# A two-block transformer on one core: attention one turn deeper, and the queries' projection ahead of the key compression

## What is computed

```python
def shared_kv(h, positions, kv_norm, kv_w, kc_pe, vc_pe, kc_w1, kc_w2, vc_w1, vc_w2, kc_gain, ks_gain, kw_gain):
    hn = rms_norm_2(h, kv_norm)
    parts = (hn @ kv_w).reshape(B, T, 6, N_KV_GROUPS, HEAD_DIM_2)
    ...
    def compress(raw, pe, w1, w2):
        blk = raw[:, idx] + pe[None, None, :, None, :]
        blk = jnp.moveaxis(blk, 3, 2).reshape(B, n_cmp, N_KV_GROUPS, CMP_LEN * HEAD_DIM_2)
        return jax.nn.gelu(blk @ w1) @ w2
    kc = compress(kc_raw, kc_pe, kc_w1, kc_w2)
    vc = compress(vc_raw, vc_pe, vc_w1, vc_w2)
    kc = partial_rope(rms_norm_2(kc, kc_gain), positions[:, ends])
    ks = partial_rope(rms_norm_2(ks, ks_gain), positions)
    kw = partial_rope(rms_norm_2(kw, kw_gain), positions)
```

## Time and profile before

| | us |
|---|---|
| median of 3 executions | 2927.88 (2927.32 to 2928.37) |
| profiled execution, its own time | 2929.42 |
| its span in the profile | 2927.6 |
| PE busy in the span | 2418.8 (83%) |
| DVE busy | 1984.4 (68%) |
| ACT busy | 1416.6 (48%) |
| PE's share of the chain that ended last | 59% |
| PE's mean granted clock, share of full | 0.879 |

### The profile page before, as it was taken

How to read it: one execution, slowest core, us unless ns; L and a number is a source line. 1 busy time by engine, 2 the same in 40 slices (tenths; PEclk the granted TensorE clock), 3 DMA queues, 4 the chain that set the end, 5 groups by cost and what they waited for, 6 DMA issues and landing times.

```text
span 2927.6 us, 31365 instructions
## 1 busy us (share of the span) xinstructions
PE 2418.8 (83%) x12811; PEld 2054.3 (70%) x12811; DVE 1984.4 (68%) x2430; ACT 1416.6 (48%) x1367; POOL 28.0 (1%) x52
## 2 busy tenths in 40 slices
PE   4837799883575999999999999968569985667898
PEld 3736699762554888888888888856459975544898
DVE  6555744656464888888888888865448865444787
ACT  5322443432332777777767777753344332244442
POOL 0000000000000000000000000000000000000000
PEclk9957899986677999999999999989689985666999
DMA  8400755741042999999999999983114541200453
GB/s 328 162 1 24 243 184 186 271 149 53 1 156 84 365 347 346 355 356 358 356 355 340 355 357 355 356 264 121 52 66 159 187 152 59 96 1 24 148 186 113
DMA packets 293719, 590.72 MB, mean 202 GB/s; under 512 B 11702, under 2 KB 86564, under 8 KB 292928
## 3 DMA queue, kind: packets, MB, share of 16 engines
q1 hardware_dynamic: 289872, 572.33, 55.0%
q0 software_dynamic: 3696, 16.32, 1.8%
HBM read 587.56 MB, written 1.05 MB: 201 GB/s over the span
## 4 chain that ended last, share of the span: by engine, by line
PE 59%; DVE 6%; ACT 1%; DMA 1%; issue 1%; POOL 0%; DVEq 0%; SPq 0%; ACTq 0%
PE ps L1108 17%; PE ps L1110 17%; PE ps L1109 17%; PE ps L1188 2%; PE ps L1173 1%; PE ps L1310 1%; DVE arena L1760 1%; DVE arena L1616 1%; PE ps L1293 1%; PE ps L1271 1%; DVE arena L1784 1%; PE ps L1145 1%; PE ps L1162 1%; PE ps L1211 1%; DVE Z L1625 0%
## 5 line engine op out<-in xcount | busy, mean ns | idle before, releaser
L778 ACT ACTIVATE w_hi<-raw 128x2048 fp32r<-128x2048 f32 x548 | 1041.9, 1907 | 621.5 <-PE ps L1110 507.3
L1601 DVE TENSOR_TENSOR w_lo<-raw,w_hi 128x2048 fp32r<-128x2048 f32 x548 | 1224.9, 2274 | 54.4 <-ACT w_hi L778 38.2
L1108 PE MATMUL ps<-w_hi,xT_hi 128*128 128x512 f32 (+3 forms) x1600 | 636.7, 398 | 43.2 <-DVE xT_lo L1706 24.8
L1110 PE MATMUL ps<-w_hi,xT_lo 128*128 128x512 f32 (+3 forms) x1600 | 623.0, 389 | 0.0
L1109 PE MATMUL ps<-w_lo,xT_hi 128*128 128x512 f32 (+3 forms) x1600 | 622.7, 389 | 0.0
L1108 PEld LDWEIGHTS ps<-w_hi,xT_hi 128*128 128x128 f32 x1600 | 306.2, 191 | 109.9 <-DVE xT_lo L1706 26.2
L1109 PEld LDWEIGHTS ps<-w_lo,xT_hi 128*128 128x128 f32 x1600 | 306.6, 192 | 62.1 <-issue 3.3
L1110 PEld LDWEIGHTS ps<-w_hi,xT_lo 128*128 128x128 f32 x1600 | 305.8, 191 | 62.3
L1108 PE MATMUL ps<-xT_hi,w_hi 128*128 128x256 f32 (+1 forms) x1120 | 323.6, 289 | 15.3 <-DVE xT_lo L2292 11.0
L1109 PE MATMUL ps<-xT_lo,w_hi 128*128 128x256 f32 (+1 forms) x1120 | 323.3, 289 | 0.0
L1110 PE MATMUL ps<-xT_hi,w_lo 128*128 128x256 f32 (+1 forms) x1120 | 323.2, 289 | 0.0
(11 more groups left out here) (314 smaller groups left out, 1970.6 us busy)
## 6 DMA issues: line engine op xcount, KB each, us to landing
raw<-in_moe_w_gate SPq DMA_DIRECT2D x112, 1024.0 KB, 5.3
raw<-in_moe_w_up SPq DMA_DIRECT2D x112, 1024.0 KB, 5.3
raw<-in_moe_w_down SPq DMA_DIRECT2D x112, 1024.0 KB, 5.3
raw<-in_w_ada SPq DMA_DIRECT2D x48, 1024.0 KB, 5.1
raw<-in_f_w_up SPq DMA_DIRECT2D x44, 1024.0 KB, 5.0
raw<-in_f_w_down SPq DMA_DIRECT2D x22, 1024.0 KB, 4.8
raw<-in_w_in SPq DMA_DIRECT2D x20, 1024.0 KB, 5.7
raw<-in_a_w_in SPq DMA_DIRECT2D x12, 1024.0 KB, 5.1
```

The lines of the kernel that those rows point to most:

```text
L778: act.activation(w_hi[:, k % HI, 0:LEN[k]], raw[:, r, 0:LEN[k]], ACT.Copy).then_inc(w_hi_ready, 1)
L1108: pe.matmul(out_, lh, rh, start=start, stop=False)
L1110: return pe.matmul(out_, ll, rh, start=False, stop=stop)
L1601: dve.tensor_tensor(w_lo[:, k % RAW, 0:LEN[k]], raw[:, k % RAW, 0:LEN[k]], w_hi[:, k % HI, 0:LEN[k]].bitcast(F32), ALU.subtract).then_inc( ...
```

## The change

**Attention.** On all engines the transposes, copies, sums and outputs of a turn come one step later, with the scores where they were. Head parts at the very beginning (`lead`: 2 in the forgetting attention, 1 in the sparse one) are transposed and copied ahead of the loop. The sparse attention gets `attP2d` as a buffer of its own in place of the scratch for the queries' squares. The clamp of the sums at 1 stays only for "few".

```diff
 # PE
-                for k in range(n + 3):
-                    if 0 <= k - 2 < n:
-                        transposed(k - 2)
+                for i in range(at.lead):
+                    transposed(i)
+                for k in range(n + 4):
+                    if at.lead <= k - 3 < n:
+                        transposed(k - 3)
                     if k < n and at.parts[k][0] != "heads":
                         scores(k)
-                    if 0 <= k - 3 < n and at.parts[k - 3][0] != "heads":
-                        sums(k - 3)
+                    if 0 <= k - 4 < n and at.parts[k - 4][0] != "heads":
+                        sums(k - 4)
 # ACT
-                    if 0 <= k - 2 < n:
-                        copies(k - 2)
-                    if k >= 4 and at.last[k - 4]:
-                        out_high(k - 4)
+                    if at.lead <= k - 3 < n:
+                        copies(k - 3)
+                    if k >= 5 and at.last[k - 5]:
+                        out_high(k - 5)
 # DVE
-                    ts(total, total, 1.0, ALU.max)
+                        ts(total, total, 1.0, ALU.max)
...
-                    if k >= 4 and at.last[k - 4]:
-                        out_low(k - 4)
+                    if k >= 5 and at.last[k - 5]:
+                        out_low(k - 5)
```

```diff
-                 "fa_in", "fa_out", "conv0", "kv", "kc", "vc", "nsa_in", "nsa_out", "conv1"]
+                 "fa_in", "fa_out", "conv0", "kv", "nsa_in", "kc", "vc", "nsa_out", "conv1"]
 # POOL
             gain_row(a["kv_norm_2"])
+            load(gain_n, a["b_norm_2"][0].partition_broadcast(P), ld_gain)
...
-            gain_row(a["b_norm_2"][0])
 # PE
             linear("kv")
+            to_columns(H, bank=4)
+            def raw_columns():
+                pe.wait_ge(dup_ready, got(dup_ready))
...
+            def key_columns():
+                pe.wait_ge(heads_ready, got(heads_ready))
...
+            linear("nsa_in", between={0: raw_columns, 1: key_columns})
...
                 for part in range(2):
                     hi, lo = slot(8)
-                    for c in range(2):
-                        for k in range(8):
-                            lpair = 8 * part + k
-                            last = three(ps[:, 4 + c, 0:2 * N_CMP], hi[:, k, c * P:(c + 1) * P],
-                                         lo[:, k, c * P:(c + 1) * P], bh[:, lpair, :], bl[:, lpair, :],
-                                         lpair == 0, lpair == 15)
+                    for k in range(8):
+                        lpair = 8 * part + k
+                        last = three(ps[0:2 * N_CMP, (6, 4)[i], 0:256], bh[:, lpair, :], bl[:, lpair, :],
+                                     hi[:, k, :], lo[:, k, :], lpair == 0, lpair == 15)
+                    last.then_inc(w_used, 1)
 # ACT
+            upto(BASE["nsa_in"] + 4)
+            copy_heads(kvT.rearrange("p n t -> p (n t)"), [(4, 512), (5, 512)], P)
+            for i in range(2):
                 act.wait_ge(blk_ready, got(blk_ready))
+                act.activation(blk_hl[i][0], blk32[i].rearrange("p l n -> p (l n)"), ACT.Copy).then_inc(blk_hi, 1)
 # DVE
+            gains[0] += 16
             norm(False)
+            for b in range(TB):
+                stt(H[:, b, :], X[:, b, :], rstd[:, b:b + 1], gain_n, ALU.mult, ALU.mult)
+            linear("kv", into_rows(zk))
+            to_columns(bank=4)
...
+            linear("nsa_in", into_rows(zn), between={0: blocks})
...
+            tt(mix[:, :, :], z[:, :, 0:D], z[:, :, 0:D], ALU.mult)
+            step(dve.tensor_reduce(stat_a, mix[:, :, :].rearrange("p b (h d) -> p (b h) d", d=HD), AX.X, ALU.add))
+            upto(BASE["vc"] + 1)
+            inv_root(stat_a, stat_a, HD)
+            for b in range(TB):
+                scale = stat_a[:, HEADS2 * b:HEADS2 * b + HEADS2]
+                tt(q[:, b], q[:, b], scale.unsqueeze(2).to_broadcast([P, HEADS2, HD]), ALU.mult)
+                tt(q[:, b], q[:, b], nqg.unsqueeze(1).to_broadcast([P, HEADS2, HD]), ALU.mult)
+            rope_of(q, cos2, sin2, nrope)
+            upto(BASE["vc"] + 1 + 2)
+            dve.wait_ge(cmp_out, got(cmp_out))
```

More of the change, by code:

```diff
@@ L458, in build @@
         ar.at = b2 + 2048
-        nq_sq = ar(1024)
-        nrope = [ar(256) for _ in range(4)]
+        attP2d = ar(1024)
+        ar(1024)
         nqT = [ar(512), ar(512)]
@@ L1110, in three, with linear @@
                 return pe.matmul(out_, ll, rh, start=False, stop=stop)
-            def linear(name, blocks=TB, cond=False):
+            def linear(name, blocks=TB, cond=False, between={}):
                 f = gi = 0
@@ L1564, in _ @@
-            z = zrows(NSA_DIM)
+            pe.wait_ge(kc_normed, got(kc_normed))
+            for g in range(2):
+                last = pe.transpose(ps[:, 1, g * 16:g * 16 + N_CMP],
+                                    kc_twice[:, g].rearrange("p s d -> p (s d)"), ident[0:N_CMP, 0:N_CMP])
+            last.then_inc(kc_tr, 1)
+            pe.wait_ge(kc_sb, got(kc_sb))
             pe.wait_ge(heads_ready, got(heads_ready))
@@ new lines, in _ @@
+            for i in range(2):
+                for side in range(2):
+                    step(dve.tensor_copy(
+                        rawdup[i].rearrange("p b (g s d) -> p b g s d", g=2, s=2)[:, :, :, side, :],
+                        blocked_rows(zk[:, :, i * P:(i + 1) * P], 2)))
+            beat().then_inc(dup_ready, 1)
+            dve.wait_ge(dup_ready, sent(dup_ready))
+            keys = [blocked_rows(zk[:, :, c0:c0 + P], 2) for c0 in (256, 512)]
+            for i, x in enumerate(keys):
+                tt(kv_sq[:, i], x, x, ALU.mult)
```

297 lines of the change are left out of this document (152 added, 145 removed).

## The result

| | before | after |
|---|---|---|
| median, us | 2927.60 (2923.31 to 2928.37, 4 runs) | 2795.45 (2792.28 to 2797.14, 4 runs) |
| span of the profiled execution | 2927.6 | 2794.5 |
| PE's mean granted clock | 0.879 | 0.902 |

The ratio is 0.955, 95% interval 0.9534 to 0.9567. The forecast was 2794.4, so the sum met the result within 1.1 us. Not all of its terms met theirs, and that is what the experiments are about.

The account below looks back on a forecast made before the run. It took circles of waits, chiefly PE's transposes on DVE's scaling, and stages waiting in sequence as the bound. Gains 46 + 11 + 7 + 69.5 = 133.5 off 2929.4, the median 1.5 lower: 2794.4 us; range 2780 to 2812, chance 0.63.

Parts of the forecast that it names:

- Part 2: Shared projection's end to sparse attention: queries' projection ahead of the compression, attention starting at 69.4 for 141.0, gain 71.6 us.
- The gain loads: Shared norm, which now waits for two gain loads instead of one: cost 2 us, between nothing and 4.1.
- Sparse attention: One turn deeper, its 24 turns shrink from 133.5 us to 87: gain 46, bounds 26 and 61.
- so PE becomes the bound there: Deeper attention at the low clock: circles of 3.8 and 4.4 us per turn, shorter than PE's 5.8.
- The third rival: Deeper turn does not overlap: ACT's circle closes in one turn, 8.8 us; attention gains nothing, 2858 us; chance 0.05.
- The 87: Sparse attention's forecast length in us, taken below 92.5 because the clock follows PE's work.
- Forgetting attention: Eight scored turns among eight head transposes, waits overlapping from the second pair on: gain 11 us, 5 to 18.
- First block: Its two attentions, four turns each: third scores no longer wait for the first scaling; gain 3.5 each, 7 us.
- The rule against part 1: Deeper attention: transposes do not count for the clock, so with a third of PE's work uncounted it would stay low.
- The first rival: Clock stays low in attention: sparse attention 108 us, gain 25.5, total 2823 us; chance 0.14.
- Clock high throughout: ACT and DVE then bound the sparse attention at 72 us, gain 61.5, total 2769 us; chance 0.13.
- Nothing in the rows shows a full PE staying low for long: Ground against a slower kernel, where dense stages' clock fails to rise, costing up to 220 us; chance 0.01.

Follow-up runs that it names:

- e3: Changed kernel with the compression's first layer as before (weights stationary, 30 columns moving, 192 small matmuls): 2820.70 us.
- e5: Changed kernel with ACT's rounding of the blocks moved ahead of its copies of the key columns: 2796.36 us.
- e6: Changed kernel with ACT's copy of turn k-3 ahead of the exponentials of turn k-1 in each attention step: 2782.63 us.
- e13: Changed kernel with ACT's copy of transposed weights in the sparse attention made twice, first into spare memory: 2806.37 us, one run.
- e1: Kernel before with only the attention's hunks (one turn deeper, clamp only for the 15-key turns): 2874.13 us.
- e2: Changed kernel with the attention's hunks taken back, so only the new order ahead of the sparse attention: 2852.61 us.
- e14: e8 with each transpose of softmax weights issued twice, in the sparse attention alone: 2781.57 us.
- e8: e7 with ACT's copies ahead of the exponentials in the attentions: 2779.49 us.
- e7: e5 with DVE's squares and sums of the queries moved between the second and third group of the queries' projection: 2793.60 us.
- e12: Changed kernel with every transpose of softmax weights issued twice, in all attentions: 2795.86 us, one run.
- e4: Changed kernel with all transposes inside the three attentions issued as plain matmuls with the identity: 2795.41 us.

## Why the prediction was right, step by step

- **Part 2, walked along the order.** The steps that set the end held to about a microsecond. Counted from the end of the shared projection (2404.7), the queries' projection began at 3.9 (forecast 4.2), the raw transposes at 14.9 (15.1), the key transposes at 27.3 (27.3), the 48-column group at 31.9 after 3.6 idle (32.2 after 3.8), that group took 9.5 (10.2), DVE was done at 63.9 (65.0) and the attention began at 68.2 (69.4). PE's 96 matmuls of the compression took 13.5, inside the 11.5 to 20.5; the second layer, off the path, began at 55.7 where the walk said about 60. `e3` shows that their form was needed, `e5` that the wait came from where the text put it. The order of instructions with durations of the old trace was enough.
- **The gain loads.** Forecast 2. The chain of waits has the load that ends last start 0.5 later and take 1.1 longer than in the earlier trace rows:

```profile
2373.45 0.52 POOL Z L707
2373.98 5.17 DMA Z<-in_b_norm
```

  The stretch around it became 1.1 us longer.
- **Sparse attention, 42.1 where I had 46.** The gain's mechanism was right: PE's waits for the scaling went from 41.0 to none in the list. The step that failed is the sentence that both circles are shorter than PE's 5.8 us, "so PE becomes the bound there", with the waits that this leaves out. The circle through ACT was in the prediction, with the copy behind the exponentials and over two turns, and that is how it runs. But I priced it for wide turns only and held it against PE's work in wide turns at the low level. Two thirds of the turns are narrower, and in the pass shown above, at the full clock, the circle takes 4.7 us against 3.4 of PE's work. The term thus lacked the 13.3 us that PE waits for ACT's copies. `e6` (7.7 us back by the order of two calls) and `e13` (11.2 us for 15.0 of ACT's work) show that these waits count. The third rival, in which the circle closes in one turn and the gain vanishes, did not come. The 87 was moreover a choice between 72 and 108, and 92.5, my figure without a faster clock, lies nearer to the 91.4. The clock share, 0.74, was inside the "0.7 or more". One small sum of mine is off and used nowhere: four exponentials of 0.51 and a copy of 1.02 are 3.1 us, not 3.3.
- **Forgetting attention, 7.5 where I had 11.** With the same code it took 64.2 us at a clock of 0.75 in the changed kernel and 67.5 at 0.63 in `e1`:

```profile
2079.90:2147.40 67.50, 53.16 (x272) 42.67 (x272) 22.51 (x97) 32.93 (x90) 0.00 (x0) 0.63 0.00 1
```

  All profiled kernels with this attention and ACT's order took 64.0 to 67.5 us, and `e2`, which has the old attention, took 69.5 where the kernel before took 71.7. So the gain is 2 to 8 us, no pair reaches the 11, and the lower bound of 5 was met by some pairs only. What failed is that "from the second pair on the waits overlap". The waits for DVE's scaling went, but others came in their place. PE's wait for the scaling before, and its two largest waits inside the stage of the changed kernel:

```profile
PE ps L1173 <- DVE arena L1784: 17.6, 7, 2.9
```

```profile
PE ps L1194 <- ACT Z L906: 6.2, 2, 3.9
PE ps L1194 <- ACT arena L913: 5.0, 4, 2.4
```

  PE waits for ACT's copies, of head sets (L906) and of weights (L913), where it had waited for DVE.
- **First block, 8.0 where I had 7.** Right in size.
- **The sum.** The two attentions gave 7.4 less than forecast, part 2 with its loads 2.1 more, the first block 1.0 more, and stages that nobody touched gave 3.8. That the total came within 1.1 us is therefore partly luck; the terms themselves were off by up to 4.
- **The rule against part 1.** The clock in the sparse attention rose from 0.62 to 0.74, and from 0.80 to 0.96 when only transposes were added (`e14` against `e8`). The first rival, the clock low throughout and 2823 us, did not come. The Trainium skill, TensorE: Matmul & The Clock Gate, Part 4: PE-mode transpose, says that the full clock does not engage for transposes; the measurement differs and decides: in this stage they count.
- **The rivals.** "Clock high throughout" (2769) did not come: at 0.93 and even 0.96 the stage was 89.4 and 82.4 us, since the circles through ACT and DVE set it. Its premise, that a high clock would bring 72, was wrong too: ACT's busy time plus 8 leaves out what ACT itself waits for.
- **"Nothing in the rows shows a full PE staying low for long."** My own had it: 20.5 of 20.6 us busy at 0.50, in the compression before. `e3` shows it for 40.8 us.

## What to carry to other kernels

When a software pipeline is made one turn deeper, write down, for each engine on the circle, the place of the instruction in that engine's own queue, and add what stands ahead of it. Do this sum for every kind of turn and at both clock levels, and hold it against PE's work in the same turns: here the wide turns at the low level said "PE", and the narrower ones at the full clock said "ACT". The order of two calls on ACT was worth 7.7 us of the sparse attention. Where a matmul moves few columns, try the few as the stationary side: here the same products took 13.5 us in place of 40.8. And a wait that is removed at one place must be looked up again at the next: `e5` and `e6` each moved theirs and kept 4.2 and 7.7 us of the stage; `e7` gained nothing, because its work was put behind the wait that it was to fill.

## What the runs showed of the hardware that I had not expected

- Transposes can raise TensorE's granted clock: 0.80 to 0.96 in the sparse attention by 128 more of them, at no cost in time (`e14` against `e8`). In the forgetting attention of `e12`, 48 more did not.
- A PE that is full for 40.8 us with matmuls that move 30 columns stayed at 0.50 from end to end (`e3`).
- Identical code in the forgetting attention differed by 3.3 us between profiled executions of two kernels, along with its clock share (67.5 us at 0.63 and 64.2 at 0.75). Whole times of one kernel spread over 5 to 17 us, so gains under some 5 us were read from a stage's window.
- A plain fp32 matmul with the identity stands in the trace as two matmul instructions where the transpose stands as one (608 against 464 in the sparse attention, `e4`).
